# One trunk layer on one core: four modulation chunks and five side loads moved behind the v projection, the activations behind the second weight chunk

## The reference

```python
sh_m, sc_m, gt_m, sh_f, sc_f, gt_f = modulation(c, w_ada, b_ada)     # silu(c) @ w_ada + b_ada, in 6 pieces
h = rmsnorm(x, g_mix) * (1.0 + sc_m) + sh_m
z = h @ w_in                       # 1024 -> pool 512 | q 512 | k 512 | v 512 | gate_a 1024 | gate_b 1024
a = pool_mixer(u_pool, w_pool, pool_scale) @ w_pa
o = attend(q, k, v) @ w_pb
x = x + gt_m * ((sigmoid(ga) * a + sigmoid(gb) * o) @ w_out)
x = x + gt_f * moe(rmsnorm(x, g_ffn) * (1.0 + sc_f) + sh_f)          # 32 experts, top 4, 402 MB of weights
y = rmsnorm(x, g_final)
```

## Time and profile before

| what | value |
|---|---|
| median of 3 runs | 1195.63 us (1194.5 to 1197.3) |
| profiled execution, own time | 1197.87 us |
| its span on the core | 1196.0 us (1.87 us lie around it) |
| PE busy | 1082.1 us, 90% of the span |
| DVE, ACT, POOL busy | 285.6, 164.4, 56.2 us |
| chain that ended last | PE 53%, DMA 31%, DVE 9% |
| read from HBM | 457.51 MB |

### The profile page before, as it was taken

One profiled execution on the slowest core, in us unless ns is written; L12 is line 12 of the kernel. 1 busy time (PEld: TensorE's weight loads), 2 busy tenths in 40 slices (PEclk: granted clock), 3 DMA queues, 4 the chain that ended last, 5 costly groups with the idle time before them and its releaser, 6 DMA issues.

```text
span 1196.0 us, 13483 instructions
## 1 busy us (share of the span) xinstructions
PE 1082.1 (90%) x5379; PEld 523.5 (44%) x5379; DVE 285.6 (24%) x582; ACT 164.4 (14%) x293; POOL 56.2 (5%) x86
## 2 busy tenths in 40 slices
PE   5997999999999999998999899999899889898986
PEld 3753998453333433343434333333334333343332
DVE  3041867332020202020202021211112021303024
ACT  2011424121011101010101011101110111011002
POOL 2137000000000000000000000000000000000000
PEclk9998999999999999999999999999999999999998
DMA  9997563879999999999999999999999999999991
GB/s 328 406 317 283 184 225 117 336 300 429 408 427 428 430 430 427 429 427 427 429 430 430 427 429 429 428 427 429 430 430 427 430 429 427 428 429 430 428 425 42
DMA packets 46869, 459.47 MB, mean 384 GB/s; under 512 B 4429, under 2 KB 4489, under 8 KB 20121
## 3 DMA queue, kind: packets, MB, share of 16 engines
q1 hardware_dynamic: 45592, 455.12, 91.2%
q0 software_dynamic: 1024, 3.29, 1.1%
q10 hardware_dynamic: 224, 0.69, 0.2%
HBM read 457.51 MB, written 1.57 MB: 384 GB/s over the span
## 4 chain that ended last, share of the span: by engine, by line
PE 53%; DMA 31%; DVE 9%; issue 5%; ACT 1%; SPq 1%; DVEq 0%; POOLq 0%; POOL 0%; ACTq 0%
DMA ring<-in_w_up_dram 28%; PE ps L1474 20%; PE ps L1436 15%; PE ps L1157 3%; PE ps L1365 2%; DMA ring<-in_w_in_dram 2%; DVE arena L991 2%; DVE arena L1027 2%; DVE arena L1018 2%; PE ps L1173 1%; PE ps L1461 1%; PE ps L1188 1%; PE ps L1190 1%; PE ps L1189 1%; DVE arena L1029 1%
## 5 line engine op out<-in xcount | busy, mean ns | idle before, releaser
L1436 PE MATMUL ps<-ring,arena 128*64 128x512 f32 x2048 | 459.3, 602 | 33.2 <-DMA ring<-in_w_up_dram 33.0
L1436 PEld LDWEIGHTS ps<-ring,arena 128*64 128x64 f32 x2048 | 159.9, 139 | 311.0 <-issue 306.6
L1474 PE MATMUL ps<-ring,arena 128*64 128x512 f32 x1024 | 238.8, 626 | 4.2 <-ACT arena L661 3.6
L1474 PEld LDWEIGHTS ps<-ring,arena 128*64 128x64 f32 x1024 | 83.1, 145 | 150.5 <-issue 150.5
L980 DVE COPY cur<-tab 128x8 f32 (+1 forms) x17 | 2.9, 171 | 449.1 <-PE ps L1396 449.1
L1016 DVE TENSOR_SCALAR arena<-ps 128x512 f32<-128x512 f32 x32 | 20.6, 686 | 304.3 <-PE ps L1436 304.3
L1396 PEld LDWEIGHTS ps<-arena 128*128 128x128 f32 x528 | 65.9, 196 | 21.8 <-issue 19.2
L1396 PE MATMUL ps<-arena 128*128 128x128 f32 x528 | 69.2, 284 | 1.0 <-DVE arena L984 1.0
L653 ACT ACTIVATE arena<-arena 128x512 f32<-128x512 f32 x32 | 19.6, 630 | 313.2 <-DVE arena L1016 313.2
L1404 PE MATMUL ps<-arena 128*128 128x512 f32 x128 | 59.2, 605 | 0.0
L641 ACT ACTIVATE arena<-ps 128x512 f32<-128x512 f32 x33 | 19.7, 597 | 245.7 <-PE ps L1396 245.7
(11 more groups left out here) (227 smaller groups left out, 770.5 us busy)
## 6 DMA issues: line engine op xcount, KB each, us to landing
ring<-in_w_up_dram SPq DMA_DIRECT2D x128, 2048.0 KB, 24.2
ring<-in_w_down_dram SPq DMA_DIRECT2D x64, 2048.0 KB, 24.6
ring<-in_w_in_dram SPq DMA_DIRECT2D x16, 1024.0 KB, 12.5
ring<-in_w_ada_dram SPq DMA_DIRECT2D x16, 1024.0 KB, 15.2
ring<-in_w_ada_dram SPq DMA_DIRECT2D x16, 512.0 KB, 11.8
ring<-in_w_out_dram SPq DMA_DIRECT2D x4, 1024.0 KB, 7.3
ring<-in_w_pa_dram SPq DMA_DIRECT2D x2, 1024.0 KB, 7.3
ring<-in_w_pb_dram SPq DMA_DIRECT2D x2, 1024.0 KB, 9.4
```

What stands on the lines that cost most here:

```text
L1436: ins = mm(ps[CAP * a:CAP * a + CAP, n, :], xgT[:, h, kk, CAP * a:CAP * a + CAP], w[a][:, at + n * HALF:at + (n + 1) * HALF], start=False, ...
L1474: ins = mm(ps[CAP * a:CAP * a + CAP, YB + n, :], hT[:, f, CAP * a:CAP * a + CAP], w[a][:, (f % 4) * D + n * HALF:(f % 4) * D + (n + 1) * H ...
```

## The change

- ("ada", 2, 4) to ("ada", 2, 7) move in `MIX` from before ("in", 4, 0) to behind gate 4's and gate 5's chunks. PE uses two after the transpose of k and two after `project_gate(5)`, as an accumulation of their own that DVE adds to the first half (`mod_rows` has one more call). Slots are given anew; ("in", 3, 1) now takes the slot of ("ada", 2, 1).
- POOL does the eight selects first, then waits until ("in", 3, 1) has landed, and only then issues the second batch of side loads.
- The two transfers of x are issued after the second "first" chunk. PE runs 16 matmuls on `ident` ahead of the first rows, transposes x between the third and the fourth chunk, and runs two `keep_busy` in place of four; the two early `cleared` stand ahead of `first_columns`.
- `prob_t` and `pt_out` use banks 4, 6, 4; `spread(0)` waits for the third evacuation (`PT_read` 3) in place of the second.

```diff
-MIX += [("in", 3, 0), ("in", 3, 1)] + [("ada", 2, k) for k in range(4, KB)]
-MIX += [("in", j, h) for j in range(4, 8) for h in range(2)]
+MIX += [("in", 3, 0), ("in", 3, 1)] + [("in", 4, h) for h in range(2)] + [("ada", 2, 4), ("ada", 2, 5)]
+MIX += [("in", 5, h) for h in range(2)] + [("ada", 2, 6), ("ada", 2, 7)]
+MIX += [("in", j, h) for j in range(6, 8) for h in range(2)]
...
+    slots[AT["in", 3, 1]:] = [5, 0, 1, 2, 3, 4, 5, 0, 1, 2, 3, 0, 1, 4, 5, 2, 3, 0, 1, 11, 12]
...
-            sp.dma_start(x[:, 0, :], A_x_prompt[0]).then_inc(L["x0"], 16)
-            sp.dma_start(x[:, 1, :], A_x_sample[0]).then_inc(L["x1"], 16)
+                if c == 2:
+                    sp.dma_start(x[:, 0, :], A_x_prompt[0]).then_inc(L["x0"], 16)
+                    sp.dma_start(x[:, 1, :], A_x_sample[0]).then_inc(L["x1"], 16)
...
+            c_after = AT["in", 3, 1]
+            pool.wait_ge(pro_loaded[mix_slot[c_after]], 16 * mix_held[c_after])
+            for q in range(3):
+                part_load(bup[32 * q:32 * q + 32, :], A_b_up[0], L["bup"])
...
             normalise(1, Ss, TOK)
+            dve.wait_ge(row_ready, 4)
+            mod_rows(2, 7, KB - 1, modrow[:, 2, :])
...
+            pe.wait_ge(vec_c, 1)
+            for _ in range(16):
+                mm(ps[:, 1, 0:P], ident[:, :], ident[:, :], start=True, stop=True)
             pe.wait_ge(silu_ready, 2)
             first_rows(0, range(2))
+            pe.wait_ge(const_ready, 2)
+            cleared(0)
+            first_rows(0, range(2, 3))
...
-            first_rows(0, range(2, 4))
+            first_rows(0, range(3, 4))
             pe.wait_ge(const_ready, 3)
-            first_columns(0)
-            keep_busy(4, 1)
-            cleared(0)
             pe.wait_ge(xr_ready, 2)
             cleared(4)
+            first_columns(0)
+            keep_busy(2, 6)
...
             ins.then_inc(pool_done, 1)
-            modulation(2, 7, range(4, KB))
...
             ins.then_inc(k_t, 1)
+            modulation(2, 7, range(4, 6), first=4)
             project_gate(5)
+            modulation(2, 7, range(6, KB))
             pe.wait_ge(prob_ready, 1)
-            pe.wait_ge(knew_ready, 1)
-            prob_t(Sp, 6)
+            pe.wait_ge(mx_ready, 2)
+            prob_t(Sp, 4)
...
                 if n == 0:
-                    pe.wait_ge(PT_read, 2)
+                    pe.wait_ge(PT_read, 3)
```

More of the change, by code:

```diff
@@ L34 @@
 RING0 = 9
-RING1 = 6
 NARROW = 27
@@ L61, in place_mixing @@
 def place_mixing():
-    slots = [c % RING0 if c < NARROW else (c - NARROW) % RING1 for c in range(len(MIX))]
-    slots[AT["in", 4, 0]:] = [5, 0, 1, 2, 3, 4, 0, 1, 2, 3, 4, 5, 0, 1, 11, 12]
+    slots = [c % RING0 for c in range(len(MIX))]
+    slots[AT["in", 3, 1]:] = [5, 0, 1, 2, 3, 4, 5, 0, 1, 2, 3, 0, 1, 4, 5, 2, 3, 0, 1, 11, 12]
     before = [max((b for b in range(c) if slots[b] == slots[c]), default=None) for c in range(len(MIX))]
@@ L414, in _ @@
             pool.wait_ge(bias_copied, 1)
[L415 to L420, removed]
             for r in range(2):
@@ L431, in _ @@
             pool.sem_inc(bias_ready, 1)
+            c_after = AT["in", 3, 1]
+            pool.wait_ge(pro_loaded[mix_slot[c_after]], 16 * mix_held[c_after])
+            for q in range(3):
+                part_load(bup[32 * q:32 * q + 32, :], A_b_up[0], L["bup"])
+            part_load(vc.rearrange("p (h d) -> p h d", h=HEADS), A_cache_v[0, 0].rearrange("h l d -> l h d"), L["vc"])
+            part_load(gffn, A_g_ffn.to_broadcast([P, D]), L["gffn"])
+            part_load(wrt[:, :, :], A_w_router[0].rearrange("(k p) n -> p k n", p=P), L["wrt"])
+            part_load(brt[:, :], A_b_router.to_broadcast([P, E]), L["brt"])
             pool.wait_ge(L["bup"], 48)
@@ L556, in pt_out @@
                 act.wait_ge(PT_done, n + 1)
-                bank = (6, 4, 6)[n]
+                bank = (4, 6, 4)[n]
                 dst = (PTp, PTs[:, 0], PTs[:, 1])[n]
@@ L747, in _, with mod_rows @@
                 V.tensor_scalar(xn[:, t, :], x[:, t, :], rstd[:, t:t + 1], None, ALU.mult).then_inc(xn_ready, 1)
-            def mod_rows(m, bank):
-                dve.wait_ge(pro_used, AT["ada", m, KB - 1] + 1)
+            def mod_rows(m, bank, last, bias):
+                dve.wait_ge(pro_used, AT["ada", m, last] + 1)
                 dve.wait_ge(L["bada"], 128)
-                V.tensor_tensor(modrow[:, m, :], ps[:, bank, :], bada[:, m - 1, :], ALU.add).then_inc(row_ready, 1)
+                V.tensor_tensor(modrow[:, m, :], ps[:, bank, :], bias, ALU.add).then_inc(row_ready, 1)
             for hf in range(2):
@@ L795, in _ @@
             ins.then_inc(pooled_ready, 1)
-            mod_rows(1, 6)
+            mod_rows(1, 6, KB - 1, bada[:, 0, :])
             dve.wait_ge(pro_used, NARROW - 1)
@@ L822, in split @@
                 ins.then_inc(unit_ready, 1)
-            mod_rows(2, 7)
+            mod_rows(2, 7, 3, bada[:, 1, :])
             split(0)
@@ L1114, in _, with modulation @@
             tp(ps[:, 7, 0:VEC], vecs[:, :], ident[0:VEC, 0:VEC]).then_inc(vec_t, 1)
-            def modulation(m, bank, ks):
+            def modulation(m, bank, ks, first=0, last=KB - 1):
                 for kk in ks:
@@ L1121, in modulation @@
                         ins = mm(ps[32 * q:32 * q + 32, bank, :], cs[:, kk, :], w[:, q * HALF:(q + 1) * HALF],
-                                 start=(kk == 0), stop=(kk == KB - 1))
+                                 start=(kk == first), stop=(kk == last))
                     ins.then_inc(pro_used, 1)
@@ L1245, in _ @@
             pe.wait_ge(kcT_ready, 1)
-            modulation(2, 7, range(4))
+            modulation(2, 7, range(4), last=3)
             project_v()
@@ L1268, in _ @@
             ins.then_inc(k_t, 1)
+            modulation(2, 7, range(4, 6), first=4)
             project_gate(5)
+            modulation(2, 7, range(6, KB))
             pe.wait_ge(prob_ready, 1)
-            pe.wait_ge(knew_ready, 1)
-            prob_t(Sp, 6)
+            pe.wait_ge(mx_ready, 2)
+            prob_t(Sp, 4)
             project_gate(6)
             pe.wait_ge(prob_ready, 2)
-            prob_t(Ss[:, :, 0:P], 4)
+            pe.wait_ge(knew_ready, 1)
+            pe.wait_ge(row_ready, 5)
+            prob_t(Ss[:, :, 0:P], 6)
             project_gate(7)
             pe.wait_ge(PT_read, 1)
-            prob_t(Ss[:, :, P:TOK], 6)
+            prob_t(Ss[:, :, P:TOK], 4)
             def spread(n):
```

## The result

| kernel | median us | ratio to the kernel before, 95% interval | profiled execution | span |
|---|---|---|---|---|
| before | 1195.63 | | 1197.87 | 1196.0 |
| after | 1205.14 (1204.93 to 1208.17) | 1.0083 [1.0062, 1.0105] | 1205.28 | 1203.4 |

The change makes the kernel slower by 0.8%. The forecast was 1198.2 us with a range of 1187 to 1204: the side was right, the size was not, and the time lies 1.1 us outside the range. The two profiled executions differ by 7.4 us of span.

What follows compares the result with a forecast made beforehand. The prediction took the mixing part's chain of waits, its longest link v's w_in transfer (25.18 us), as what to shorten, the expert part's queues being full. -8.1 - 3.0 + 9.9 + 3.6 + 0.2 = +2.6 on 1195.63 gave 1198.2 us, range 1187 to 1204.

Steps and rivals of the forecast that it cites:

- v's chunk early: Ahead of `project_v`: without side loads in front, v's chunk lands at 90.0 instead of 98.1, 8.1 us gained.
- low clock in `project_v`: In `project_v`: some 1.6 us of its 15.77 are low clock and stay in; bounds 0 and 1.6 gained.
- modulation chunks out: Between `project_v` and the gates: four modulation chunks no longer stand ahead of the scores, 3.0 us gained.
- POOL's split beside DVE: Behind `project_v`: POOL's late split of b_up and DVE's splits exclude each other, 9.9 us lost, bounds 0 and 15.7.
- modulation chunks back: Between gate units: the four chunks' work returns where PE is 96% busy, 3.6 us lost, bound 2.6.
- `spread(0)`: Small term: it waits for the third evacuation and can't fill the wait for it, 0.2 us lost.
- first stage: Start of the mixing part: any earlier end goes into the wait for v's chunk, 0, bounds 1 either way.
- POOL gets its turn: Rival: POOL gets a turn after each DVE operation and b_up lands late; +6.3, 1201.9 us; chance 0.16.
- The cover: Behind `project_v`: 3.4 us of DVE's PSUM-input work and 0.5 of PE's slack lie beside POOL's 13.8.
- The forecast's bound of 15.7 for POOL: Upper bound of POOL's loss: 13.8 + 1.9 if b_up lands at 101.4 and nothing lies beside POOL.
- POOL costs little: Rival: POOL's split hardly delays DVE behind `project_v`; sum -7.3, 1188.3 us; chance 0.27.
- v not early: Rival: the queue holds v's chunk, which lands at about 94 to 96; +5.7, 1201 us; chance 0.07.

Runs made afterwards that it cites:

- kernel 2: The changed kernel with all five side loads issued at their old place, behind bias_copied and ahead of the selects: 1198.28 us, 1.0011.
- kernel 5: The changed kernel with b_up's three transfers and POOL's split moved up behind w_pool's load, the other four side loads late: 1196.48 us, 1.0003.
- kernel 8: The kernel before with the first stage's edits alone (x's loads later, sixteen warm-up matmuls, new order): 1196.53 us, 1.0005.
- Kernel 4: The kernel before with only the second batch of side loads moved behind v's chunk: 1201.73 us, 1.0037.
- kernel 1: The changed kernel without POOL's seven instructions that split b_up (expert bias left out): 1190.93 us, 0.9943.
- Kernel 11: The changed kernel with eight filling matmuls on PE ahead of `project_v`: 1203.65 us, 1.0069.
- kernel 12: The changed kernel without the three subtractions of POOL's split, its four casts kept (split not computed): 1193.12 us, 0.9975.
- kernel 3: The changed kernel with only b_up's three transfers issued at their old place, the other four side loads late: 1201.80 us, 1.0034.
- kernel 9: Kernel 6 with b_up's three transfers made one transfer to 96 partitions: 1211.36 us, 1.0122.
- kernel 6: The kernel before with b_up's transfers and split behind w_pool's load and the other four side loads behind v's chunk: 1192.80 us, 0.9978.
- kernel 7: Kernel 5 with eight filling matmuls on PE ahead of `project_v`: 1193.65 us, 0.9986.
- kernel 10: Kernel 7 with b_up's three transfers made one transfer to 96 partitions: 1206.84 us, 1.0086.

## Why the prediction was wrong

The differences of the two traces, in the order of the prediction's sum (the first gate unit is at 122.19 and 123.92, the router's first matmul at 236.66 and 243.82):

| step | predicted | measured | from |
|---|---|---|---|
| v's chunk early | -8.1 | -8.5 | first matmul 98.22, 89.69 |
| low clock in `project_v` | 0 | +1.3 | 15.77, 17.04 |
| modulation chunks out | -3.0 | -3.1 | 8.20, 5.14 in kernels 2 and 5 |
| POOL's split beside DVE | +9.9 | +13.6 | 17.19 - 5.14, and 1.5 in the gate units |
| modulation chunks back | +3.6 | +3.9 | 114.47, 118.37 in kernels 2 and 5 |
| `spread(0)` | +0.2 | in the row above | |
| first stage | 0 | 0 | kernel 8 |
| behind the router | 0 | +0.2 | router to end |
| sum | +2.6 | +7.4 | |

**v's chunk: right in size.** Kernel 4 has the move of the side loads alone: first matmul at 89.41. In the changed kernel the last wait is another, that for the new slot: free at 83.96, not at 85.6, and 5.6 us to landing make 89.55. The forecast's 90.0 fits both paths; that they end within 0.3 us of each other is chance.

**The first stage: right**, and for the reason given.

**The modulation chunks: right**, both ways; their move costs 0.8 us, and no run shows a gain from it.

**POOL's split: the step that failed.** The mechanism is the one forecast, no sharing in either direction, and the first kernel shows that it carries the whole loss. The term was mis-sized: 9.9 us, where 13.6 are lost. The sum was POOL's work that is left when DVE's begins, less what can lie beside it: 13.8 - 3.4 - 0.5. Both parts went wrong on the same side, by 1.8 and 1.7 us:
- The start. The prediction took the median to landing (8.5 us, first cast 99.5) and set 101.4 as its bound; the first cast came at 102.62, 12.8 us after the issue. The split needs the last of the three transfers, and that one took 11.7 us (the median was 9.3). So at 106.81, when DVE's L807 was ready, 1.84 of the first subtraction and all that follows were left: 1.84 + 2 x 4.05 + 3 x 1.88 = 15.6 us, not 13.8. The rival *POOL gets its turn* said that b_up would decide it "if b_up lands after about 100", and that is what happened.
- The cover. 3.4 us of PSUM-input work and 0.5 of slack were to lie beside POOL. DVE's stretch from L807 to the end of the second split takes 20.7 us, 7.3 in the kernels 1, 2 and 5: 13.4 more, so only 2.2 of the 15.6 were covered. They are L755 (0.68) and 0.2 to 0.5 us at each change of turn, where the rows overlap. L832 and L838 stand behind splits in DVE's order, and the splits waited; they ran at 127.39 and 128.72, after POOL was done. Work can cover only what its own engine lets it reach.

Kernel 11 bears this out: there L807 is ready at 102.97, 18.6 us of POOL's work are left, and the stretch takes 23.5 us, 16.2 more than 7.3, so 2.4 are covered. That POOL too was stretched (22.9 us for its lone 19.7) is DVE's work between its instructions and costs DVE nothing more; the prediction expected POOL's end at about 126, and it was 125.5. The 0.2 left up to 13.6 are not traced further.

```profile
89.11 15.67 PE L1173 MATMUL ps<-ring 128*128 128x512 f32 x32 [4.23 <-DMA ring<-in_w_in_dram]
```

By these two the prediction's "as before" was right, and the length of the wait (8.15 us before, 4.05 after) does not set the loss. Whether the other executions of after have the 17.04 too, no trace tells. A second, unforeseen share lies in the gates: after PE's wait of 9.8 us the first unit's matmuls start 0.21 us apart, later ones 0.12; this is inside the 1.5 us above.

**The range.** The forecast's bound of 15.7 for POOL stands 5.8 above its 9.9, which gives 1204.0, the range's end; no loss at the clock was added to it. Of the 6.9 us between 1198.2 and 1205.14 the table explains 4.8. The other 2.1 are the executions compared: the profiled one of before is 2.2 us above its median, that of after is 0.1 above its own. In the runs beside the experiments the kernel before has medians of 1195.7 to 1196.8.

**The rivals.** *POOL costs little* is refuted by kernels 1, 4 and 12. *v not early* is refuted by v's 89.69. *POOL gets its turn and b_up lands late* was the nearest, 1201.9, and its point of decision was met; it too adds only 1.7 us of POOL's work to the 9.9 and keeps the cover of 3.4 + 0.5.

## What to carry to other kernels

When a load is moved, follow the instructions that wait for it: here 1.7 MB out of the way of one chunk gained 8.5 us and took a 20 us split of POOL from an idle stretch of DVE into the one that the gates wait for. When two engines exclude each other, the loss is the other's work that is still left, less only what your engine can reach in its own order; the start must be taken from the last transfer, not from the median; and an in-order engine needs its waits in the order of its work (kernel 3). Measure what a transfer does to the others while it is in flight, not only its bytes.

## What the runs showed of the hardware

- POOL's casts and subtractions on 32 partitions and DVE's SBUF-to-SBUF casts and subtractions take strict turns, a whole instruction each; DVE's pair of casts went from 0.75 to 5.70 us.
- While b_up (32 rows, read three times) is in flight full queues move about 240 GB/s (243 from 82.0 to 86.6 in kernel 3, 237 in kernel 5, 240 in kernel 9), and 386 to 427 once it has landed; the first three us of the flight in kernel 3 still ran at 421. As three transfers it landed in 12.4 us in the median (kernel 6), as one of 96 partitions in 34.7 (kernel 9), and the whole traffic stayed slow so long.
- PE's idle wait ahead of `project_v` was followed by six us at a lower granted clock in ten of the eleven traces without filling matmuls: 8.15 us by 0.70 (before), 4.05 by 0.50 (after), 4.23 by 0.72 (kernel 1), 4.06 by 0.72 (kernel 5), 2.87 by 0.72 (kernel 4), 2.40 by 0.73 (kernel 9). Only the sixth kernel, with 2.28 us, kept 1.00, as did all three with the filling (kernels 7, 10 and 11).
